# A hybrid decoder step on one core: the first token gather of each layer split into two gathers of 64 slots

## What is computed

```python
def _moe(h, router_w, router_bias, p):
    scores = jax.nn.sigmoid((ht @ router_w).astype(jnp.float32))
    ...
    expert_idx = g_idx * EXPERTS_PER_GROUP + local
    ...
    def expert_block(args):
        xb, e = args
        return (jax.nn.silu(xb @ p["e_gate"][e]) * (xb @ p["e_up"][e])) @ p["e_down"][e]
    ...
    contrib = (ys[dest] * wts.reshape(A)[order][:, None]).astype(ht.dtype)
    out = jnp.zeros((T, D), ht.dtype).at[tok].add(contrib)
```

## Time and profile before

| | us |
|---|---|
| median of three runs | 1857.2 |
| the three runs | 1857.2, 1861.19, 1853.19 |
| the profiled execution | 1857.72 |
| its span, first to last instruction | 1855.9 |
| PE busy | 1536.3 (83%) |
| DMA moved | 567.56 MB, 306 GB/s over the span |
| mean granted PE clock | 0.906 |

### The profile page before, as it was taken

How to read it: one execution, slowest core, us unless ns; L and a number is a source line. 1 busy time by engine, 2 the same in 40 slices (tenths; PEclk the granted TensorE clock), 3 DMA queues, 4 the chain that set the end, 5 groups by cost and what they waited for, 6 DMA issues and landing times.

```text
span 1855.9 us, 29639 instructions
## 1 busy us (share of the span) xinstructions
PE 1536.3 (83%) x11826; PEld 844.1 (45%) x11826; DVE 744.7 (40%) x1706; ACT 331.8 (18%) x775; POOL 117.0 (6%) x168
## 2 busy tenths in 40 slices
PE   5999999999866667677889999999996677677785
PEld 2765543546433333334366555355553334333442
DVE  0353565767402222122534256586652222122226
ACT  1225321203100000000123442120310000001001
POOL 4000002200200000000020000221000000000000
PEclk9998999989988888888889899998998888888888
DMA  9453447558999999999963642745799999999994
GB/s 325 165 182 141 127 128 211 164 196 338 416 412 427 428 428 429 428 428 428 355 231 137 231 125 85 203 151 207 299 370 427 428 429 428 428 428 429 428 427 188
DMA packets 94857, 567.56 MB, mean 306 GB/s; under 512 B 8278, under 2 KB 9054, under 8 KB 69171
## 3 DMA queue, kind: packets, MB, share of 16 engines
q1 hardware_dynamic: 82866, 532.05, 70.9%
q0 software_dynamic: 11904, 34.34, 6.6%
HBM read 550.55 MB, written 15.81 MB: 305 GB/s over the span
## 4 chain that ended last, share of the span: by engine, by line
PE 53%; DMA 39%; DVE 3%; issue 2%; ACT 1%; SPq 1%; DVEq 1%; ACTq 0%
DMA ring<-in_exp_w_up 38%; PE ps L1551 10%; PE ps L1019 9%; PE ps L994 9%; PE ps L1389 3%; PE ps L1241 3%; PE ps L1001 2%; PE ps L858 2%; DMA ring<-in_w_ada 1%; PE ps L1519 1%; PE ps L1210 1%; PE ps L1145 1%; PE ps L1186 1%; PE ps L916 1%; PE ps L1375 1%
## 5 line engine op out<-in xcount | busy, mean ns | idle before, releaser
L1551 PE MATMUL ps<-ring,xTb 128*32 128x256 f32 x4224 | 325.8, 477 | 221.6 <-DMA ring<-in_exp_w_up 218.8
L1551 PEld LDWEIGHTS ps<-ring,xTb 128*32 128x32 f32 x4224 | 161.8, 136 | 384.6 <-issue 339.0
L2771 DVE TENSOR_TENSOR hb<-sg,ps 128x128 f32<-128x128 f32 x66 | 25.0, 379 | 458.0 <-ACT sg L1956 458.0
L1019 PE MATMUL ps<-ring,hT 128*128 128x512 f32 x384 | 171.4, 598 | 0.0
L994 PE MATMUL ps<-hT,ring 128*128 128x288 f32 x640 | 164.5, 416 | 4.8 <-DVE hT L2121 2.5
L1519 PE MATMUL ps<-sel,h_tm 128*128 128x128 f32 (+1 forms) x912 | 163.3, 306 | 0.3 <-DVEq L2695 0.3
L1519 PEld LDWEIGHTS ps<-sel,h_tm 128*128 128x128 f32 x912 | 124.6, 189 | 53.7 <-issue 21.8
L994 PEld LDWEIGHTS ps<-hT,ring 128*128 128x128 f32 x640 | 122.1, 194 | 42.7 <-issue 8.1
L1568 PE MATMUL ps<-ring,hTb 128*32 128x256 f32 x2048 | 126.6, 389 | 3.3 <-DVEq L2774 2.5
L1956 ACT ACTIVATE sg<-ps 128x128 f32<-128x128 f32 x66 | 18.3, 278 | 612.6 <-PE ps L1551 612.6
L1019 PEld LDWEIGHTS ps<-ring,hT 128*128 128x128 f32 x384 | 71.0, 190 | 98.8 <-issue 98.3
(11 more groups left out here) (502 smaller groups left out, 1668.3 us busy)
## 6 DMA issues: line engine op xcount, KB each, us to landing
ring<-in_exp_w_gate SPq DMA_DIRECT2D x66, 2048.0 KB, 18.8
ring<-in_exp_w_up SPq DMA_DIRECT2D x66, 2048.0 KB, 23.3
ring<-in_exp_w_down SPq DMA_DIRECT2D x64, 2048.0 KB, 24.8
ring<-in_w_ada SPq DMA_DIRECT2D x24, 2048.0 KB, 10.0
ring<-in_w_in SPq DMA_DIRECT2D x22, 2048.0 KB, 9.0
ring<-in_w_out SPq DMA_DIRECT2D x8, 2048.0 KB, 9.2
h0s<-in_state_ssd POOLq DMA_DIRECT2D x16, 512.0 KB, 7.2
out_ssd_s<-h0s POOLq DMA_DIRECT2D x16, 512.0 KB, 5.3
```

The source lines that it names most:

```text
L1019: last = mm(o[:, :], hT[:, k, T0[i]:T0[i] + P], w[:, k, :], start=(k == 0), stop=(k == KT - 1))
L1551: last = mm(ps[32 * j:32 * j + 32, b, 0:2 * P], xTb[:, k, m * BLK:(m + 1) * BLK], w[:, 0:2, k * D_EXPERT + j * P:k * D_EXPERT + (j + 1) * ...
```

## The change

The first gather of each layer is made for slots 0 to 63 alone, in the new function `gather_part` with 64 moving columns instead of 128. The gather of slots 64 to 127 is a second call, placed in `first_quad` behind gate and up of block 1. ACT takes each part with `take_part`, half as wide as `take_gather`. The first part has signals of its own (`front_full`, `front_taken`); the second uses the old ones, and PE waits for `g_taken` before the next quad's gather writes the same banks.

```diff
+        front_full, front_taken = sig("first_slots_full", 2), sig("first_slots_taken", 2)
...
+                def gather_part(lo, hi, c):
+
+                    for k in range(lo, hi):
+                        at = (k % 4) * QS + c
+                        for i in range(NT):
+                            last = mm(ps[:, 6 + k // 4, at:at + 2 * BLK], h_tm[0:ROWS[i], i, k * P:(k + 1) * P],
+                                      sel[0:ROWS[i], i, c:c + 2 * BLK], start=(i == 0), stop=(i == NT - 1))
+                    return last
+
...
-                gather(0, 4, QS).then_inc(gq_full.sem, 1)
-                gather(4, 8, QS).then_inc(gq_full.sem, 1)
+                gather_part(0, 4, 0).then_inc(front_full.sem, 1)
+                gather_part(4, 8, 0).then_inc(front_full.sem, 1)
...
-                        if k == KT // 2 and second_half is not None:
-                            pe.wait_ge(g_taken, second_half)
+                        if k == KT // 2 and second_half:
+                            pe.wait_ge(front_taken.sem, front_taken.at(l, 2))
...
-                    pe.wait_ge(g_half.sem, g_half.at(l, 1))
+                    pe.wait_ge(front_taken.sem, front_taken.at(l, 1))
                     idle["pe"].stand(pe)
-                    gate_up(d0, 0, 0, steady + 1)
+                    gate_up(d0, 0, 0, True)
                     gate_up(d0, 1, 1)
+                    gather_part(0, 4, 2 * BLK).then_inc(gq_full.sem, 1)
+                    gather_part(4, 8, 2 * BLK).then_inc(gq_full.sem, 1)
...
                     pe.wait_ge(sel_ready, steady + 2)
+                    pe.wait_ge(g_taken, steady + 1)
                     gather(0, 4, QS).then_inc(gq_full.sem, 1)
...
+                def take_part(half, c):
+                    return cp(xTb[:, 4 * half:4 * half + 4, c:c + 2 * BLK],
+                              ps[:, 6 + half, :].rearrange("p (k t) -> p k t", k=4)[:, :, c:c + 2 * BLK])
+
...
-                act.wait_ge(gq_full.sem, gq_full.at(l, 1))
-                take_gather(0)
-                act.wait_ge(gq_full.sem, gq_full.at(l, 2))
-                take_gather(1)
+                act.wait_ge(front_full.sem, front_full.at(l, 1))
+                take_part(0, 0).then_inc(front_taken.sem, 1)
+                act.wait_ge(front_full.sem, front_full.at(l, 2))
+                take_part(1, 0).then_inc(front_taken.sem, 1)
...
                         for b in range(2):
                             silu(d0, b)
+                        act.wait_ge(gq_full.sem, gq_full.at(l, 1))
+                        take_part(0, 2 * BLK).then_inc(g_half.sem, 1)
+                        act.wait_ge(gq_full.sem, gq_full.at(l, 2))
+                        take_part(1, 2 * BLK).then_inc(g_taken, 1)
```

More of the change, by code:

```diff
@@ L1539, in _, with gate_up @@
                 idle["pe"].stand(pe)
-                def gate_up(d, b, m, second_half=None):
+                def gate_up(d, b, m, second_half=False):
                     w = (ring, ring1)[b]
```

## The result

The changed kernel takes 1877.1 us (median of 4 runs, 1875.81 to 1881.5) against 1855.6 us before (median of 4, the three of the table ahead and 1854.08): ratio 1.0111, 95% interval 1.0085 to 1.0136. All ratios here compare undisturbed executions alone; one of 3428 us, of before_mixed, is left out. The forecast of 1858.5 us was wrong, and the range missed the time. Of the named cases E, the fallen clock, comes nearest; the prediction had given it 2%.

What follows compares the result with a forecast made beforehand. The DMA stream of expert weights was taken as the bound in the expert phases. An earlier start (-0.84 us) and a hole (+1.5) gave +0.66 us a layer, +1.3 for two: 1858.5 us, range 1853 to 1864.

Steps and rivals of the forecast that it cites:

- E: PE at 1.2 GHz from expert 2's issue on, in each layer: up to +33 us, 1891; chance 0.02.
- What bounds the kernel: Expert phases of both layers: the DMA stream is the bound; its start and whether it runs dry count.
- reserve: DMA stream before expert 4's gate: 6.1 us of added PE work is borne before a hole opens.
- Part 1: First gather narrowed to 64 slots: 7.60 us instead of 8.44, stream starts sooner, gain 0.84 us a layer.
- e2: Issue of expert 2's gate, after the first gather: claimed 0.84 us sooner, 457.78 instead of 458.62.
- Part 2: Other 64 slots gathered behind gate and up of block 1: +7.60 us on PE, gate of 4 at 483.82.
- The hole: DMA stream runs dry before expert 4's data: about 1.5 us in each layer, bounds nothing and 2.4 us.
- its rule: Hole at expert 4: its gate's issue behind expert 2's, plus 1.73 us start-up, less 26.3 us of stream.
- `down` of 3: SP's queue: issue moves from 469.09 to 475.85, hidden by 8.39 MB queued ahead until about 480.
- Rival B: At expert 4's issue the hole closes, only the earlier start is left: -1.7 us, 1855.5 us; chance 0.28.
- C: First gather scales with its columns, 4.22 us, no hole: -8.4 us, 1848.8 us; chance 0.04.
- D: Both gathers at 176 ns a record, nothing shortened, 8.44 us added, hole 2.3: +4.7 us, 1861.9; chance 0.10.

Runs made afterwards that it cites:

- before_mixed: Kernel before, with products of block 0 for features k = 0 and 1 put between the first gather's steps 4 to 7; ratio 1.0025.
- second_mixed: Changed kernel with first gather 128 columns wide and the second, 64 wide, mixed into gate and up of block 1; ratio 1.0071.
- wide_both: Changed kernel's order, but both gathers move all 128 columns of the selection; ratio 1.0029.
- before_fill12: Kernel before, with 12 wide filler matmuls between gate and up of block 1 and the row broadcasts; ratio 1.0071.

## Why the prediction was wrong, point by point

- **What bounds the kernel: right.** The stream of expert weights, its start and its reserve decided every variant.
- **Part 1, the gather gets 0.84 us shorter: this step failed.** The 158 ns a record were right for full clock, and second_mixed shows them in this phase. The error was to carry them from a row of 24 to a row of 48 and to call the clock given. The narrow gather took 9.97 us instead of 7.60, and the products behind it 2.3 us more, so e2 came 3.8 us later, not 0.84 sooner.
- **Part 2, +7.60 us: mis-sized.** The second gather took 9.07 us (469.73 to 478.80), and broadcasts and `down` ran at the low clock after it: from there to the next gather 478.80 to 488.34 = 9.54 us, where it had been 7.03 (461.94 to 468.97). Gate of 4 at 30.02 instead of 26.04.
- **The hole: right in kind, and its rule in size.** Fed with what was measured, it gives 30.02 + 1.73 - 26.3 = 5.4; with 3.8 for the start 9.2 us a layer, against 9.0 and 8.3 in the streams. It opens in two steps, at both windows of 164 GB/s. The first is at `down` of 3, which the prediction had called hidden: it was issued 22.07 us behind gate of expert 2 (10.47 before), its data could run at 23.8, and the four matrices ahead of it last 1.73 + 4 x 4.9 = 21.3 us. Rival B (no hole) falls: wide_both and before_fill12 both paid. C falls with the rate. D, both gathers at 176 ns with the clock held, is wide_both: 1861.9 forecast, and the ratio of 1.0029 on 1857.2 is 1862.6.
- **Rival E: the right cause with the wrong chance, and at another place.** It let the clock be low from expert 2's issue on; the clock fell before that, in the first gather, was back at 465 us, and fell again in the second. It was dismissed with "PE pauses less after the change". That takes a pause for the only thing that lowers the clock. The trace of the kernel before already held a warning, in a stretch that the prediction didn't look at, the router. PE in order of time, and windows with the clock:

```profile
429.67 1.60 PE L1446 MATMUL ps<-rw,hT 128*128 128x32 f32 x24
431.76 2.00 PE L1446 MATMUL ps<-rw,hT 128*128 128x32 f32 x16 [0.49 <-ACT hT L1914]
433.56 3.68 PE L1456 MATMUL ps<-con,hT 128*128 128x128 f32 x17
```

```profile
428.00:432.00 4.00, 3.51 (x38) 2.86 (x37) 3.50 (x15) 3.58 (x9) 0.00 (x0) 1.00 1.03 442
432.00:434.00 2.00, 2.00 (x18) 2.00 (x18) 0.99 (x3) 0.15 (x2) 0.00 (x0) 0.88 0.95 410
434.00:436.00 2.00, 2.00 (x12) 1.75 (x11) 1.05 (x5) 1.19 (x4) 0.00 (x0) 0.50 1.01 426
```

There PE works on products of 32 moving columns, from 431.76 us on without a gap, and the clock reads 0.50 right behind them. It is a weaker case than the gathers, since PE paused for 0.49 us just ahead and was busy for 3.51 of the 4 us of the first window. A clock of 1.00 in the old rows of a stretch holds for the old instructions alone.

## What to carry to other kernels

Before you narrow the moving side of a row of matmuls, ask two things of the trace: whether the record gets shorter at all (here 10%, as the weight load stays), and whether the same row elsewhere was long enough to show what it does to the clock. A share of 100% busy says nothing on that; look for stretches of narrow matmuls and read the granted clock behind them, and if a narrow row must be long, mix it with wide work. And where a DMA stream is the bound, compute its reserve at each release: work inside it is free, as 4.3 us of pure filler were here, and work beyond it was paid once in each layer.

## What was not expected of the hardware

- PE's clock fell from 1.00 to 0.50 with PE busy 100%, some 4 to 6 us into a row of gather matmuls of 64 or 96 moving columns, in every such gather of five kernels; with 128 columns (48 records in 8.44 us) it never did, nor with 64 when products of 256 columns stood between (second_mixed).
- 96 columns cost more than 64, once the clock had fallen: 10.77 us against 9.97 for the first gather.
- Outside the expert phases a piece of the time moved by up to 6.7 us between two executions of one program, largely with PE's clock, while the phases bound by DMA repeated within 0.6 us. Differences of a few us are better read from the stretches than from the total.
